# The first norm of a two-block network: the first slab and the input land and are split in quarters by input chunk, the squares and the mean come behind the next slab, and TensorE multiplies zeros until the first products

## What is computed

```python
def rms_norm(x, g):
    xf = x.astype(jnp.float32)
    y = xf * lax.rsqrt(jnp.mean(xf * xf, axis=-1, keepdims=True) + RMS_EPS)
    return (y * g.astype(jnp.float32)).astype(x.dtype)

def swiglu(x, w1, w3, w2):
    return (jax.nn.silu(x @ w1) * (x @ w3)) @ w2

h = h + 0.5 * swiglu(rms_norm(h, ffn1_norm[l]), ffn1_w1[l], ffn1_w3[l], ffn1_w2[l])
```

## Time and profile before

| | |
|---|---|
| median of 3 runs | 1950.24 us (1949.57 to 1953.35) |
| profiled execution | 1953.1 us, of it 1951.1 us span from the first to the last instruction |
| busy in the span | TensorE 1917.8 us (98%), VectorE 1097.3 (56%), ScalarE 733.4 (38%), GpSimd 23.7 (1%) |
| granted TensorE clock, mean of the span | 0.997 |
| DMA | 173.43 MB, mean 89 GB/s |

### The profile page before, as it was taken

One profiled execution on the slowest core, in us unless ns is written; L12 is line 12 of the kernel. 1 busy time (PEld: TensorE's weight loads), 2 busy tenths in 40 slices (PEclk: granted clock), 3 DMA queues, 4 the chain that ended last, 5 costly groups with the idle time before them and its releaser, 6 DMA issues.

```text
span 1951.1 us, 23956 instructions
## 1 busy us (share of the span) xinstructions
PE 1917.8 (98%) x9314; PEld 1610.4 (83%) x9314; DVE 1097.3 (56%) x1281; ACT 733.4 (38%) x828; POOL 23.7 (1%) x30
## 2 busy tenths in 40 slices
PE   6999999999999999999999999999999999999998
PEld 5888888888778888888888888888888888888886
DVE  5343445677665665434355655455555876555656
ACT  4222233335353333222232243333335644344445
POOL 0000000000000000000000000000000100000000
PEclk9999999999999999999999999999999999999999
DMA  4222222411212222222222322222222221222122
GB/s 167 101 89 104 81 87 90 149 65 49 81 35 85 103 104 91 89 105 88 92 89 98 139 87 87 86 86 86 84 82 71 76 85 67 87 86 78 73 86 65
DMA packets 27447, 173.43 MB, mean 89 GB/s; under 512 B 3200, under 2 KB 3232, under 8 KB 10368
## 3 DMA queue, kind: packets, MB, share of 16 engines
q1 hardware_dynamic: 24912, 165.95, 24.0%
q0 software_dynamic: 1328, 4.61, 0.8%
q10 hardware_dynamic: 1152, 2.10, 0.3%
HBM read 169.50 MB, written 3.15 MB: 88 GB/s over the span
## 4 chain that ended last, share of the span: by engine, by line
PE 92%; DVE 4%; ACT 3%; issue 1%; DMA 0%; DVEq 0%; ACTq 0%
PE acc L1625 28%; PE acc L1627 28%; PE acc L1626 28%; PE att L1626 2%; PE att L1627 2%; PE att L1625 2%; ACT tmp L563 1%; DVE w_lo L920 1%; PE att L2104 1%; ACT tmp L555 1%; PE att L2103 1%; DMA h<-in_x 0%; DVE w_lo L930 0%; DVE rstd L975 0%; ACT w_hi L433 0%
## 5 line engine op out<-in xcount | busy, mean ns | idle before, releaser
L1625 PE MATMUL acc<-x_hi,w_hi 128*128 128x512 f32 x1400 | 549.8, 393 | 14.8 <-DVE w_lo L920 14.7
L1627 PE MATMUL acc<-x_hi,w_lo 128*128 128x512 f32 x1400 | 546.0, 390 | 0.0
L1626 PE MATMUL acc<-x_lo,w_hi 128*128 128x512 f32 x1400 | 545.9, 390 | 0.0
L920 DVE TENSOR_TENSOR w_lo<-raw,w_hi 128x2048 fp32r<-128x2048 f32 (+1 forms) x165 | 376.1, 2280 | 148.4 <-ACT w_hi L433 144.9
L433 ACT ACTIVATE w_hi<-raw 128x2048 fp32r<-128x2048 f32 (+1 forms) x165 | 313.4, 1899 | 117.4 <-PE acc L1627 113.7
L1625 PEld LDWEIGHTS acc<-x_hi,w_hi 128*128 128x128 f32 x1400 | 263.5, 188 | 71.9 <-DVE w_lo L920 16.1
L1626 PEld LDWEIGHTS acc<-x_lo,w_hi 128*128 128x128 f32 x1400 | 263.5, 188 | 56.3 <-issue 1.7
L1627 PEld LDWEIGHTS acc<-x_hi,w_lo 128*128 128x128 f32 x1400 | 263.4, 188 | 55.0
L482 ACT ACTIVATE tmp<-tmp 128x512 f32<-128x512 f32 x44 | 27.8, 632 | 294.0 <-DVE tmp L1010 294.0
L1625 PE MATMUL acc<-g_hi,w_hi 128*128 128x512 f32 x352 | 137.1, 390 | 0.0
L1627 PE MATMUL acc<-g_hi,w_lo 128*128 128x512 f32 x352 | 137.0, 389 | 0.0
(11 more groups left out here) (335 smaller groups left out, 2811.8 us busy)
## 6 DMA issues: line engine op xcount, KB each, us to landing
raw<-in_ffn_up SPq DMA_DIRECT2D x44, 1024.0 KB, 4.7
raw<-in_ret_head SPq DMA_DIRECT2D x24, 1024.0 KB, 4.7
raw<-in_ffn_down SPq DMA_DIRECT2D x32, 704.0 KB, 4.0
raw<-in_mix_gate SPq DMA_DIRECT2D x8, 1024.0 KB, 4.8
raw<-in_ret_out SPq DMA_DIRECT2D x8, 1024.0 KB, 4.8
raw<-in_sb_v SPq DMA_DIRECT2D x8, 1024.0 KB, 4.7
raw<-in_sb_kq SPq DMA_DIRECT2D x8, 1024.0 KB, 4.7
raw<-in_sb_g SPq DMA_DIRECT2D x8, 1024.0 KB, 4.7
```

What stands on the lines that cost most here:

```text
L920: tt(w_lo[:, slot, 0:cols], raw[:, slot, 0:cols], w_hi[:, slot, 0:cols].bitcast(F32), ALU.subtract).then_inc(w_ready, 1)
L1625: mm(dst, still[0], move[0], start=first, stop=False)
L1626: mm(dst, still[0], move[1], start=False, stop=False)
L1627: return mm(dst, still[1], move[0], start=False, stop=last)
```

## The change

The first slab is loaded, copied and subtracted in four quarters of 512 columns; a quarter holds two input chunks of both output blocks, so that its rows are 1 KB pieces (`quarter`). SP issues them in turn with chunks 2 to 7 of x; ScalarE issues the gains and chunks 0 and 1. The fetch of the second slab waits until chunk 5 of x has landed. ScalarE and VectorE take a quarter, then its two chunks of x, and so on; then slab 1, and only then the squares (now into `first_sq`, a room of eight chunks, without the turn of four) and their sums. ScalarE and VectorE leave out the `prep` of the first output in `ffn`, since slab 1 is split by then. TensorE makes five fp32 products of a zeroed place of `tmp` into `att`, which nothing reads, before its first pair; the first pair waits quarter by quarter (`first_pair`), and the mean moves from chunk 5 of the first pair to chunk 3 of the second. Blank and far context lines are left out.

```diff
--- before.py
+++ after.py
@@ -154,6 +154,9 @@
+        def quarter(v, q):
+            return v.rearrange("p (o k) -> p o k", o=2)[:, :, 2 * BLK * q:2 * BLK * (q + 1)]
         def by_chunk(v):
@@ -165,6 +168,8 @@
+        with ExitStack() as scope:
+            first_sq = sb("first_sq", [P, DC, TOK], F32, scope)
         with ExitStack() as scope:
@@ -303,6 +308,9 @@
         kv_sum = sem("kv_sum")
+        first_landed = [sem(f"first_landed{q}") for q in range(PARTS - 1)]
+        first_ready = sem("first_ready")
+        zeros_ready = sem("zeros_ready")
@@ -318,15 +326,27 @@
-            def ffn(name):
-                with loop(sp, FC // 2, (n, 2)) as i:
+            def first_slabs():
+                for q in range(PARTS):
+                    sp.dma_start(quarter(raw[:, 0, :], q), quarter(dram["ffn1_up"][0], q)).then_inc(
+                        raw_landed[0] if q == PARTS - 1 else first_landed[q], 16)
+                    for c in range(2 * q + 2, min(2 * q + 4, DC)):
+                        sp.dma_start(h[:, c, :], dram["x"][:, c, :]).then_inc(x_landed[c], 16)
+                n.next()
+                sp.wait_ge(x_landed[DC - 3], 16)
+                fetch(dram["ffn1_up"][1])
+            def ffn(name, begun=0):
+                with loop(sp, FC // 2 - begun, (n, 2)) as i:
                     for j in range(2):
-                        fetch(dram[name + "_up"][2 * i + j])
+                        fetch(dram[name + "_up"][2 * i + (j + 2 * begun)])
                 with loop(sp, DC, (n, 2)) as i:
-            ffn("ffn1")
+            first_slabs()
+            ffn("ffn1", 1)
             for g in range(N_GROUPS):
@@ -389,7 +409,6 @@
         def _(pool):
-            pool.dma_start(gains[:], dram["gains"]).then_inc(gains_landed, 16)
             for dst, name in ((pool_scale, "pool_scale"), (ident, "ident"), (mean_d, "mean_d"),
@@ -459,11 +478,6 @@
-            def square(c, src):
-                if c >= 4:
-                    act.wait_ge(ssq_ready, sq.at(c - 3))
-                nc.scalar.activation(t(c % 4), src, ACT.Square).then_inc(sq_ready, 1)
             def weigh(dst, c, gain, by_class=False):
@@ -472,10 +486,11 @@
-            def ffn(next_gain, by_class=False):
+            def ffn(next_gain, by_class=False, begun=False):
                 def up(place, first):
                     for j in range(2):
-                        prep()
+                        if not (begun and first and j == 0):
+                            prep()
                         if first and j == 0:
@@ -498,18 +513,24 @@
             hr = Count()
-            sq = Count()
-            for c in range(DC):
+            act.dma_start(gains[:], dram["gains"]).then_inc(gains_landed, 16)
+            for c in range(2):
                 act.dma_start(h[:, c, :], dram["x"][:, c, :]).then_inc(x_landed[c], 16)
             for c in range(DC):
+                if c % 2 == 0:
+                    q = c // 2
+                    act.wait_ge(raw_landed[0] if q == PARTS - 1 else first_landed[q], 16)
+                    nc.scalar.activation(quarter(w_hi[:, 0, :], q), quarter(raw[:, 0, :], q), ACT.Copy).then_inc(
+                        w_hi_ready if q == PARTS - 1 else w_part_ready, 1)
                 act.wait_ge(x_landed[c], 16)
-                square(c, h[:, c, :])
                 weigh(x_hi, c, gains[:, 0, :])
-                if c == 1:
-                    prep()
+            n.next()
+            prep()
+            for c in range(DC):
+                nc.scalar.activation(first_sq[:, c, :], h[:, c, :], ACT.Square).then_inc(sq_ready, 1)
             act.wait_ge(const_ready, 1)
-            ffn(gains[:, 1, :], by_class=True)
+            ffn(gains[:, 1, :], by_class=True, begun=True)
@@ -963,11 +984,9 @@
                 dve.wait_ge(sq_ready, squared.next())
-                if c == 0:
-                    nc.vector.tensor_copy(ssq[:], t(0)).then_inc(ssq_ready, 1)
-                else:
+                if c > 1:
                     dve.wait_ge(ssq_ready, sq.at())
-                    tt(ssq[:], ssq[:], t(c % 4), ALU.add).then_inc(ssq_ready, 1)
+                tt(ssq[:], first_sq[:, 0, :] if c == 1 else ssq[:], first_sq[:, c, :], ALU.add).then_inc(ssq_ready, 1)
                 sq.next()
@@ -1000,10 +1019,11 @@
-            def ffn(next_gain, weights=None, by_class=False):
+            def ffn(next_gain, weights=None, by_class=False, begun=False):
                 def up(place, first):
                     for j in range(2):
-                        prep()
+                        if not (begun and first and j == 0):
+                            prep()
                         if first and j == 0:
@@ -1040,18 +1060,31 @@
             nc.vector.memset(r_tok[:], 0.0).then_inc(acc_free, BANKS)
+            nc.vector.memset(t(5), 0.0).then_inc(zeros_ready, 1)
             dve.wait_ge(gains_landed, 16)
             for c in range(DC):
+                if c % 2 == 0:
+                    q = c // 2
+                    dve.wait_ge(raw_landed[0] if q == PARTS - 1 else first_landed[q], 16)
+                    if q < PARTS - 1:
+                        dve.wait_ge(w_part_ready, part.next())
+                    else:
+                        dve.wait_ge(w_hi_ready, n.at(1))
+                    tt(quarter(w_lo[:, 0, :], q), quarter(raw[:, 0, :], q), quarter(w_hi[:, 0, :], q).bitcast(F32),
+                       ALU.subtract).then_inc(w_ready if q == PARTS - 1 else first_ready, 1)
+                dve.wait_ge(x_landed[c], 16)
+                weigh(x_lo, c, gains[:, 0, :], x_hi)
+            n.next()
+            prep()
+            squared.next()
+            for c in range(1, DC):
                 sum_square(c)
-                weigh(x_lo, c, gains[:, 0, :], x_hi)
-                if c == 1:
-                    prep()
             dve.wait_ge(const_landed, 6 * 16)
             dve.wait_ge(const_ready, 1)
-            ffn(gains[:, 1, :], by_class=True)
+            ffn(gains[:, 1, :], by_class=True, begun=True)
@@ -1669,7 +1702,7 @@
                 for c in range(DC):
-                    if between is not None and c == 5:
+                    if between is not None and c == (3 if wait is None else 5):
                         between()
@@ -1686,12 +1719,31 @@
-            def ffn(adds, between):
+            def first_pair():
+                dst = bank(), bank()
+                for c in range(DC):
+                    if c == DC - 2:
+                        slab()
+                    elif c % 2 == 0:
+                        pe.wait_ge(first_ready, c // 2 + 1)
+                    pe.wait_ge(op_ready, c + 1)
+                    for o in range(2):
+                        block = slice((o * DC + c) * BLK, (o * DC + c + 1) * BLK)
+                        last = passes(dst[o], (w_hi[:, 0, block], w_lo[:, 0, block]), (x_hi[:, c, :], x_lo[:, c, :]), c == 0, c == DC - 1)
+                        if c == DC - 1:
+                            last.then_inc(seg_done, 1)
+            def ffn(adds, between, begun=False):
                 sq.next(adds)
                 op.next(DC)
-                pair(at, between)
-                pair()
+                if begun:
+                    first_pair()
+                    pair(None, between)
+                else:
+                    pair(at, between)
+                    pair()
                 op.next(2)
@@ -1714,7 +1766,11 @@
-            ffn(DC, first_mean)
+            pe.wait_ge(zeros_ready, 1)
+            for _ in range(5):
+                mm(att[:, 0, :], t(5)[:, 0:P], t(5), start=True, stop=True)
+            ffn(DC - 1, first_mean, True)
             plain = [slice(P * k, P * k + P) for k in range(TB)]
```

## The result

The changed kernel takes 1954.82 us (median of 20 runs, 1953.82 to 1955.69), the kernel before 1951.58 us in the same comparison (20 runs, 1949.26 to 1954.95). The ratio is 1.0016, with a 95% interval of 1.001 to 1.0023: slower by 3.2 us at the medians. A repeat on another occasion gave 1954.13 against 1949.78 us, ratio 1.0022 (1.0013 to 1.0031). The forecast was 1949.2 us in a range up to 1953.2.

A forecast was written before the change was run, and what follows sets the result against it. TensorE, busy 98% of the span, was taken as the bound, with its longest wait 14.7 us at the start. Third pair -2.6 us and half clock +1.6 gave -1.0 off the 1950.24 median: 1949.2 us, range 1945.5 to 1953.2.

The forecast's parts named there:

- the early start: TensorE's first real products: at 8.3 us at full clock, 6.4 us earlier, 8.8 us with the saved half clock.
- a gain of 2.6 us: TensorE's third pair: starts at 37.3 instead of 39.9 us; the rest of the 8.8 us becomes new waits.
- C: Rival at the third pair: the norm's chain does not hold TensorE, the 8.8 us stay whole, 1941.4 us; chance 0.06.
- B: Rival at the third pair: the norm's chain holds it, but the clock stays up over the gap, 1947.6 us; chance 0.15.
- D: Rival at the loads: small rows make slab 1 late, landing at 25.1 us, time 1958.9 us; chance 0.09.
- E: Rival at the start: zeros end late or do not keep the clock, third pair unmoved, 1950.2 us; chance 0.08.
- A: The forecast itself: the norm's chain holds the third pair and the clock falls, 1948.7 to 1952.2 us; chance 0.62.

The follow-up runs named there:

- the run with one wait: The changed kernel without ScalarE's own wait for the constants ahead of its ffn call: 1953.09 us, ratio 1.0011 to the kernel before.
- The extra root alone: The changed kernel with one single-column square root on ScalarE behind the squares, to load the root's table early: 1953.16 us, ratio 1.0007 to the kernel before.

## Why the prediction was wrong

What held: the early start is real; the time is set by slab 1, norm and gate up to slab 2's split; the third pair stands behind a gap; half clock follows it. The failed step is the sum of that chain, 37.3 us forecast and 40.25 measured, and within it above all the table load of the root, which was put at nothing. It turned a gain of 2.6 us into a loss of 0.4. Term by term, the first eight adding up to either sum:

| term | forecast | measured |
|---|---|---|
| slab 1's copy starts | 15.4 | 16.32 |
| `w_hi` and `w_lo` of slab 1 | 4.25 | 4.24 |
| seven sums and the casts of the constants | 5.60 | 5.79 |
| mean, from the constants on | 0.9 | 1.25 |
| table of the root | 0 | 1.28 |
| root | 0.75 | 0.81 |
| reciprocal to the end of slab 2's `w_lo` | 10.33 | 10.33 |
| TensorE behind that `w_lo` | 0.05 | 0.23 |
| half clock behind the gap | 1.6 | 2.1 (1.6 to 2.9 in other traces) |

The largest is the table load. I had written that it loads during the sums, without a row for it. In the kernel before it does start ahead of the mean's end:

```profile
24.62 1.28 ACT L460 ACT_TABLE_LOAD   x1
```

But there slab 1's split stands between the wait for the constants and the root. The change takes it away, so that two waits stand in a row before the same activation, and the load then stands behind both; the run with one wait shows it. At the start, too, the first table load begins only at 5.69 us, behind the first quarter, and the first product comes at 9.25 instead of 8.3 us. Part of this is that the products of zeros themselves end at 8.85 us; the last 0.4 us are a wait for `x_lo`, which stands behind that load and which holds the first product of the repeat by 0.97 us. That delay cost nothing at the end: the third pair waits for another chain. The second term is the late slab, 0.9 us: I took a value near the lower end of 14.9 to 17.6 us, and 1 KB rows and the wait together took it to the middle. In other executions the copy starts at 16.09 to 16.64 us. The sums' 0.73 us came from one pair of rows; here they are 0.79 us apart. The mean, behind a wait, takes 1.14 us in the chain and not 0.86.

Between the forecast of 1.0 us faster and the 3.2 us slower that were measured lie 4.2 us. They are 3.0 us of chain, 0.5 us of half clock, 0.4 us near 1122 us that no term foresaw, and some 0.3 us that are not placed. The sum was also built on a median of three runs, 1950.24 us, where twenty give 1951.58.

The rivals: C is refuted, the chain does hold TensorE. B is refuted by the clock of 0.50 behind the gap. D's mechanism is there at a tenth of its price, 0.9 of 9.7 us: from 3.5 to 13.2 us the engines move 360 GB/s where it was 398. Its line was a start of 16.4 us, and 16.32 here and 16.42 in the repeat lie on that line, so by the forecast's own count the late slab alone ate nearly the whole gain of 1.0 us. The Trainium skill (DMA: Bandwidth & Descriptors, Specifications), by which 1 KB rows go at line rate and slab 1 lands at 14.9 us, is not borne out here: without the wait on SP, slab 1 is copied right behind its landing at 16.26 us with 1 KB rows (370 GB/s from 3.5 to 13.2 us), and with whole rows it has landed before ScalarE is free at 15.53 (393 GB/s). Of E the mechanism is refuted, the zeros work; its outcome, a third pair that starts about where it did, came all the same, through the longer chain. The range's upper end, 1953.2, was A's upper bound and 1 us; it varied the slab and the clock and took every engine step as known, and the table load was such a step.

What remains open: why the drops of the clock in the middle of the kernel come in some executions only, why the half clock behind a gap lasts 8 to 14 products, and what delays VectorE near 1122 us in the changed kernel. The extra root alone also has the widest spread of the variants, 5.0 us; it goes with the mean granted clock (0.998 in the runs up to 1951.5 us, 0.995 in the slowest), but why it has so many levels is open.

## What to carry to other kernels

Before an engine's first work is moved earlier, follow what it will need next but one: here TensorE had only 2.6 us of slack against the chain that its third pair waits for, and an earlier start of 5.5 us turned into a gap and a half clock. Work that depends on data already there (a weight's split) should not stand in an engine's list behind work that waits for a long chain (a norm's root and gate); that one move was worth 7 to 8 us. Products that keep the clock up pay only where the array is the bound right after them, and a gap put in by the change itself is the place to look first. When the medians of two variants differ by less than the drops that come and go cost, the same row of both traces, taken ahead of the first drop, compares them better.

## What the runs showed of the hardware that was not expected

A table load stands ahead of its activation's wait with one wait (24.62 us before, 22.29 us in the run with one wait) and behind with two in a row (27.60, and 5.69 at the start): 1.28 us that a single line puts on the path. It need not stand behind both. At the start of the kernel before, ScalarE waits for the gains and then for chunk 0 of x, and the load runs at 5.22 us, before the gains have landed:

```profile
5.22 1.28 ACT L465 ACT_TABLE_LOAD   x1 [5.22 <-issue]
7.33 0.63 ACT L465 ACTIVATE tmp<-h 128x512 f32<-128x512 f32 x1 [0.83 <-DMA gains<-in_gains]
```

All these rows fit a load that stands behind the second of two waits in the list but not behind the first; no run was made to test that. The Trainium skill (ScalarE: Activation LUTs, What ACT_TABLE_LOAD costs) gives 1283 ns for the load and about as much again for a drain. The first agrees; of the second the traces here show nothing, as the load begun at 5.69 is followed by its activation at 6.98, and the one at 27.60 by the root at 28.90.

A 0.26 MB load in 1 KB rows, issued first of all at 0.75 us, lands 4.9 us later, while the first chunk of x in the kernel before, the same size in 2 KB rows, took 3.1. The rows alone do not explain this, since chunks 0 and 1 of x, still in 2 KB rows, take 5.3 us in the changed kernel. Firmer is the rate: with 1 KB rows in the mix the engines move 352 to 370 GB/s at full share from 3.5 to 13.2 us (eleven traces), with none 393, 397 and 401 (three).

The clock falls behind gaps much shorter than the new one (1.85 us, rows 10), but not always: in the trace of the repeat the same gap of 1.85 us, at 1597.81 us, is followed by full clock. Behind the gaps of 4.5 to 5.9 us it fell in all seven traces that have one, and the slow products lost 1.6 to 2.9 us, so that a gap of 5.9 us costs 8 to 9 us in all.
